# Expert gate and up weights loaded in 4 KB rows, tokens gathered from a plainly ordered copy, pick counts kept in PSUM, and the first refill of the weight ring split into four

## The reference, cut to what matters

```python
def ec_moe(x, w_router, w_gate, w_up, w_down):       # once per depth, DEPTH = 2
    cap = CAPACITY_FACTOR * N // N_EXPERTS            # 2 * 256 // 16 = 32
    aff = jax.nn.softmax(jnp.einsum('bnd,de->bne', x, w_router).astype(jnp.float32), axis=-1)
    gates, idx = lax.top_k(jnp.swapaxes(aff, 1, 2), cap)
    xin = x[bidx, idx]                                # 32 tokens for each of 16 experts
    h = jax.nn.silu(jnp.einsum('becd,edf->becf', xin, w_gate)) * jnp.einsum('becd,edf->becf', xin, w_up)
    out = jnp.einsum('becf,efd->becd', h, w_down) * gates[..., None].astype(x.dtype)
    return jnp.zeros_like(x).at[bidx, idx].add(out.astype(x.dtype))
```

## Time and profile before

| | |
|---|---|
| median of 3 runs | 1518.0 us (1516.62 to 1518.1) |
| the profiled execution | 1516.21 us, of which the profile's span is 1514.4 us |
| PE busy | 1277.8 us (84%) |
| PE weight load busy | 759.9 us (50%) |
| DVE, ACT, POOL busy | 515.0, 235.6 and 325.2 us |
| DMA | 498.93 MB in 88544 packets, mean 329 GB/s |
| chain that ended last | PE 48%, DMA 39%, DVE 3% |

### The profile page before, as it was taken

How to read it: one execution, slowest core, us unless ns; L and a number is a source line. 1 busy time by engine, 2 the same in 40 slices (tenths; PEclk the granted TensorE clock), 3 DMA queues, 4 the chain that set the end, 5 groups by cost and what they waited for, 6 DMA issues and landing times.

```text
span 1514.4 us, 21701 instructions
## 1 busy us (share of the span) xinstructions
PE 1277.8 (84%) x9352; PEld 759.9 (50%) x9352; DVE 515.0 (34%) x982; ACT 235.6 (16%) x490; POOL 325.2 (21%) x278
## 2 busy tenths in 40 slices
PE   8999987668667668999998667777668999999998
PEld 7555534224224234865644224324324975899943
DVE  2686111001001006676311000000002555489894
ACT  2132100001000001351300000000000144212120
POOL 2635000000000004684300000000000654375700
PEclk9999999889889889999999888879989999999999
DMA  9938899999999999845799999999999973835100
GB/s 340 385 111 353 345 427 427 427 428 426 427 428 428 426 426 370 332 167 195 270 427 426 427 428 428 427 426 427 427 427 407 344 235 112 269 121 190 62 0 28
DMA packets 88544, 498.93 MB, mean 329 GB/s; under 512 B 8677, under 2 KB 31649, under 8 KB 64129
## 3 DMA queue, kind: packets, MB, share of 16 engines
q1 hardware_dynamic: 85728, 490.23, 79.8%
q0 software_dynamic: 2720, 7.32, 1.5%
HBM read 496.45 MB, written 1.07 MB: 329 GB/s over the span
## 4 chain that ended last, share of the span: by engine, by line
PE 48%; DMA 39%; DVE 3%; another core or an unknown queue 2%; issue 1%; ACT 0%; SPq 0%; DVEq 0%
DMA weight_ring<-in_moe_w_down 19%; PE bank L950 13%; DMA weight_ring<-in_moe_w_up 10%; PE bank L953 8%; DMA weight_ring<-in_moe_w_gate 6%; PE bank L1252 6%; PE bank L1449 4%; PE bank L1304 3%; DMA phase_room<-in_moe_w_gate 3%; PE bank L1227 3%; PE bank L1319 3%; PE bank L912 2%; PE bank L1418 1%; PE bank L1175 1%
## 5 line engine op out<-in xcount | busy, mean ns | idle before, releaser
L1252 PE MATMUL bank<-weight_ring,x_tok 128*32 128x256 f32 x3328 | 225.7, 422 | 99.8 <-DMA weight_ring<-in_moe_w_up 74.6
L1252 PEld LDWEIGHTS bank<-weight_ring,x_tok 128*32 128x32 f32 x3328 | 109.6, 119 | 212.5 <-issue 84.2
L743 POOL TENSOR_TENSOR weight_ring<-weight_ring 128x512 f32<-128x512 f32 x120 | 163.2, 1390 | 182.0 <-PE bank L950 73.2
L1304 PE MATMUL bank<-weight_ring,xT 128*32 128x512 f32 x864 | 135.4, 757 | 75.6 <-DMA weight_ring<-in_moe_w_down 67.0
L732 POOL TENSOR_TENSOR weight_ring<-weight_ring 128x512 f32<-128x512 f32 x60 | 80.4, 1370 | 451.5 <-DMA weight_ring<-in_w_qkv 438.0
L2312 DVE TENSOR_TENSOR xT<-xT,bank 128x256 f32<-128x256 f32 x32 | 13.5, 421 | 437.4 <-PE bank L1252 437.4
L1319 PE MATMUL bank<-x_tok,xT 128*128 128x512 f32 x256 | 122.8, 623 | 0.0
L2319 DVE COPY x_tok<-bank 128x512 f32<-128x512 f32 x32 | 22.1, 691 | 245.0 <-PE bank L1304 245.0
L1304 PEld LDWEIGHTS bank<-weight_ring,xT 128*32 128x32 f32 x864 | 27.1, 123 | 155.4 <-DMA weight_ring<-in_moe_w_down 76.1
L773 POOL DMA_DIRECT2D phase_room<-in_gla_w_in x1 | 1.0, 953 | 429.4 <-PE bank L1304 429.4
L1319 PEld LDWEIGHTS bank<-x_tok,xT 128*128 128x128 f32 x256 | 48.2, 199 | 84.0 <-issue 84.0
(11 more groups left out here) (319 smaller groups left out, 1619.9 us busy)
## 6 DMA issues: line engine op xcount, KB each, us to landing
weight_ring<-in_moe_w_gate SPq DMA_DIRECT2D x52, 2048.0 KB, 48.4
weight_ring<-in_moe_w_up SPq DMA_DIRECT2D x52, 2048.0 KB, 49.7
weight_ring<-in_moe_w_down SPq DMA_DIRECT2D x52, 2048.0 KB, 48.9
phase_room<-in_moe_w_gate SPq DMA_DIRECT2D x12, 2048.0 KB, 47.0
phase_room<-in_moe_w_up SPq DMA_DIRECT2D x12, 2048.0 KB, 50.3
weight_ring<-in_w_up SPq DMA_DIRECT2D x22, 1024.0 KB, 10.0
phase_room<-in_moe_w_down SPq DMA_DIRECT2D x8, 2048.0 KB, 50.4
weight_ring<-in_gla_w_in SPq DMA_DIRECT2D x6, 2048.0 KB, 23.3
```

Of the source, the lines that this page charges most:

```text
L743: nc.gpsimd.tensor_tensor(b, a, b, ALU.subtract).then_inc(weights_summed[x], 1)
L1252: last = mm(bank[q * CAP:(q + 1) * CAP, 0:S], xinT[:, 4 * r + k, j * CAP:(j + 1) * CAP], w[k][:, q * S:(q + 1) * S], start=(r == 0 and k = ...
L1304: last = mm(PS[i][k * CAP:(k + 1) * CAP, :], hidT[:, 4 * r + k, :], w[k][:, i * 512:(i + 1) * 512], start=(r == 0), stop=(r == 1), skip_gr ...
```

## The change

It has one part for the loads, and four that follow from it or stand at the start of each depth of experts.

1. **Layout.** Partition p of a gate or up tile holds rows k x 128 + p of its half. A load is four pieces of 4 KB for each partition; down stays at 16 KB. `x_hat` becomes a view with contiguous chunks, and the norm's gain and bias columns come from a block that is already in SBUF (four small DVE copies early in the program), so four tiny GpSimd loads go.
2. **Pick counts.** DVE's running sum and mask work on PSUM, with a column of ones that TensorE writes by one extra multiplication.
3. **Filler.** `keep_busy` goes from 19 to 21.
4. **Residual.** ACT scales the second 128 tokens after it has taken its first two chunks of the gather, not before.
5. **First refill.** The tile with index 12 is loaded in four parts of 512 KB, each issued when TensorE has used the row that it replaces.

```diff
+T_REFILL = [TILE_BEFORE.index(base) for base in T_MOE]
...
-    x_hat = acc_t[:, :].rearrange("p (t n k) -> p t k n", t=TT, k=KC)
+    x_hat = acc_t[:, :].rearrange("p (t k n) -> p t k n", t=TT, k=KC)
...
     def arrived(pe, n):
-        pe.wait_ge(landed[SLOT_OF[n]], landings(n))
+        if n in T_REFILL:
+            pe.wait_ge(refilled, 64 * (T_REFILL.index(n) + 1))
+        else:
+            pe.wait_ge(landed[SLOT_OF[n]], landings(n))
...
+        def load_by_rows(n, src):
+
+            layer = T_MOE.index(TILE_BEFORE[n])
+            for k in range(4):
+                if k < 3:
+                    sp.wait_ge(row_used, 3 * layer + k + 1)
+                else:
+                    free(n)
+                sp.dma_start(slot(n)[:, k * D:(k + 1) * D], src[:, k]).then_inc(refilled, 16)
+            sp.sem_inc(landed[SLOT_OF[n]], 16)
...
-            ws = [t[w][layer].rearrange("e (p r k) n -> e r p (k n)", p=P, k=4)
-                  for w in ("moe_w_gate", "moe_w_up", "moe_w_down")]
+            ws = [t[w][layer].rearrange("e (r k p) n -> e r p k n", p=P, k=4) for w in ("moe_w_gate", "moe_w_up")]
+            ws.append(t["moe_w_down"][layer].rearrange("e (p r k) n -> e r p (k n)", p=P, k=4))
...
+                elif n in T_REFILL:
+                    load_by_rows(n, src)
                 elif i < E * TPE - 1:
-                    load(n, src)
+                    load(n, src, slot(n).rearrange("p (k n) -> p k n", k=4) if c < 4 else None)
...
-            for cols, of in ((gain_cols, g), (bias_cols, b)):
-                pool.dma_start(cols, of.rearrange("(p k) -> p k", k=KC)).then_inc(rows_landed, 16)
...
-                last = turn(PS[2][0:E, tt * P:(tt + 1) * P], aff[:, tt, :], ident)
-            last.then_inc(affT_done, 1)
-            keep_busy(19, PS[3], right=consts[:, 0:P])
+                turn(PS[2][0:E, tt * P:(tt + 1) * P], aff[:, tt, :], ident)
+            mm(PS[2][0:E, S:S + 1], ident[0:E, 0:E], ones[0:E, 0:1], start=True, stop=True).then_inc(affT_done, 1)
+            keep_busy(21, PS[3], right=consts[:, 0:P])
...
+                        if e == 0 and c == 0 and r == 0 and k < 3:
+                            last.then_inc(row_used, 1)
...
+            for layer in range(DEPTH):
+                v.tensor_copy(gain_of[layer], norm_cols[:, layer, 0])
+                last = v.tensor_copy(bias_of[layer], norm_cols[:, layer, 1])
...
-            link(v.tensor_tensor_scan(pick, ones[0:E, 0:1].to_broadcast([E, S]), work, 0.0, ALU.mult, ALU.add))
-            v.scalar_tensor_tensor(pick, work, 0.0, pick, ALU.is_lt, ALU.mult).then_inc(slots_ready, 1)
+            count = PS[2][0:E, 0:S]
+            link(v.tensor_tensor_scan(count, PS[2][0:E, S:S + 1].to_broadcast([E, S]), work, 0.0, ALU.mult, ALU.add))
+            v.scalar_tensor_tensor(pick, work, 0.0, count, ALU.is_lt, ALU.mult).then_inc(slots_ready, 1)
```

More of the change, by code:

```diff
@@ L249, in build_in @@
     shift = small[:, 144:146]
-    gain_cols, bias_cols = small[:, 228:236], small[:, 236:244]
+    gain_of, bias_of = (small[:, 228:236], small[:, 88:96]), (small[:, 236:244], small[:, 146:154])
     norm_blocks = room[0:24, 1056:1056 + P]
@@ L398, in build_in @@
     router_landed = sem("router_landed")
+    row_used, refilled = sem("row_used"), sem("refilled")
     router_steps, weighted_done = sem("router_steps"), sem("weighted_done")
@@ L745, in moe_small @@
         def moe_small(layer):
-            pool.wait_ge(rows_landed, 64 * (layer + 1))
+            pool.wait_ge(rows_landed, 32 * (layer + 1))
             for tt in range(TT):
@@ L1657, in moe, with residual @@
         def moe(layer, use):
-            for tt in range(TT):
+            def residual(tt):
                 act.wait_ge(row_scaled, 2 * (TT * layer + tt + 1))
@@ L1662, in moe @@
                 last.then_inc(alpha_x, 1)
+            residual(0)
             base, n0, m0 = T_MOE[layer], E * layer, NG * layer
-            act.wait_ge(rows_landed, 64 * (layer + 1))
+            act.wait_ge(router_steps, 2)
+            gain_cols, bias_cols = gain_of[layer], bias_of[layer]
             act.wait_ge(alpha_x, TT * layer + 1)
@@ L1675, in moe @@
                         last.then_inc(xin_act, 1)
+                        if e == 0 and half == 0:
+                            residual(1)
                 act.wait_ge(tile_used, base + TPE * e + 2)
@@ L1860, in layer_apply @@
                 if use % 2 == 0:
-                    dve.wait_ge(rows_landed, 64 * (use // 2 + 1))
+                    dve.wait_ge(rows_landed, 32 * (use // 2 + 1))
                 else:
@@ L2253, in rms @@
             if tt == 0:
-                dve.wait_ge(*((rows_written, sum(ROUNDS)), (rows_landed, 64 * 2 + 16), (gain_landed, 48))[u])
+                dve.wait_ge(*((rows_written, sum(ROUNDS)), (rows_landed, 32 * 2 + 16), (gain_landed, 48))[u])
             v.scalar_tensor_tensor(acc[:, tt], x_tok[:, tt], inv_spread[:, n:n + 1], gain,
@@ L2288, in moe @@
             base, n0, m0 = T_MOE[layer], E * layer, NG * layer
-            dve.wait_ge(rows_landed, 64 * (layer + 1))
+            dve.wait_ge(router_steps, 2)
+            gain_cols, bias_cols = gain_of[layer], bias_of[layer]
             dve.wait_ge(alpha_x, TT * layer + 1)
```

## The result

The changed kernel takes 1538.99 us (median of 4 runs, 1536.87 to 1539.48) against 1517.31 us (1515.83 to 1518.1) for the kernel before: a ratio of 1.0142, 95% interval 1.0128 to 1.0156. That is 21.7 us slower, where +7.8 was forecast; the direction was right, and the time lies above the range of 1517 to 1534 us. The profiled execution took 1539.07 us with a span of 1537.3, against a span of 1514.4 before.

The account below looks back on a forecast made before the run. The prediction took the experts' load stream, from tile 1's release on, as the bound: +18.4 us for 4 KB pieces and -10.6 for earlier release make +7.8, 1526 us on the median of 1518.0, range 1517 to 1534 us.

Parts of the forecast that it names:

- What bounds the kernel: Both depths' experts: the load stream counts from tile 1's release, then 414 us to the last landing, 4.99 us a tile.
- The cost: 4 KB pieces: Gate and up loads behind the stream's start: 413 GB/s, +0.167 us for each of 110 tiles, +18.4 us.
- Rival A: Expert loads: a deep queue hides the packets' overhead, only the gain is left, 1507.4 us; chance 0.14.
- Rival C: Gather: not faster, since something other than the step makes it slow; 1536 us; chance 0.05.
- Rival D: Gate and up loads: the new pieces run like 2 KB pieces, +56 us, 1563 us; chance 0.03.
- The gain: Contiguous gather and start of each depth: tile 1 free 6.05 and 4.54 us earlier, -10.6 us together.
- the forecast -0.78: Gather's start: running sum -0.91 and extra multiplication +0.13 at the first depth; only +0.13 at the second.
- The fifth edit is worth 1.3 us a depth: First refill by rows: starts 1.35 us earlier, so does not hold back the stream; 1.3 us a depth, within the 10.6.
- rival B: Gather: contiguous instructions run at half clock, 1.6 us a depth lost, 1529 us; chance 0.18.
- The filler: Router's stretch: two more products lie under DVE's pick rounds, at nothing; 0.45 us a depth if they stuck out.
- Edits at nothing: ACT's residual, filler, four DVE copies (under 1.5 us if uncovered) and dropped GpSimd loads, all put at nothing.
- The running sum: DVE before the gather: 0.68 us at both depths with one SBUF operand only, -0.91 at the first depth.

Follow-up runs that it names:

- experiments 3, 5 and 6: Changed kernel with gate and up loaded in 16, 8 and 2 KB pieces respectively, features paired wrongly: 1513.5, 1523.1 and 1570.5 us.
- pieces_16k: Changed kernel with gate and up loaded in 16 KB pieces again, features paired wrongly: 1513.5 us, ratio 0.9967.
- edits_2_to_5: Kernel before with all of the change but its layout part: 1516.76 us, ratio 0.9992.
- experiments 8 and 11: The changed kernel and the kernel of experiment 10, each with its first refill as one whole load: 1540.57 and 1512.48 us.
- gather_alone: Kernel before with contiguous x_hat in the old feature order, written permuted by ScalarE and read permuted by GpSimd; 16 KB pieces: 1516.29 us, ratio 0.9993.
- layout_only: Kernel before with the layout part of the change alone: 1540.29 us, ratio 1.0151.
- permuted_short_filler: Kernel of experiment 10 with less filler, one product for three and 14 for 21: 1509.85 us, ratio 0.9949.
- experiment 4: Changed kernel with the four gain and bias copies made by ScalarE from PSUM instead of VectorE from SBUF: 1534.31 us, ratio 1.0112.
- experiment 12: The same run as permuted_short_filler: kernel of experiment 10 with less filler in the router's stretch, 1509.85 us, ratio 0.9949.
- experiment 10: Changed kernel but with 16 KB pieces, x_hat written permuted by ScalarE and gain columns loaded by GpSimd, no VectorE copies: 1513.26 us, ratio 0.9964.

## Why the prediction was right and wrong

**What bounds the kernel: right.** The difference lies in the release of tile 1 and in the stream behind it; the rest behind the last landing is 348.8 or 348.9 us before and after the change.

**"The cost: 4 KB pieces": the mechanism right, the size too small, and this is the step that failed by most.** It is 5.1 of the 15.1 us that the forecast lacks. Alone it would have left the time at 1526 + 5.1 = 1531 us, inside the range; it took the terms below that stood at nothing, 7.6 us together, to carry it out. The forecast had 0.167 us a tile from a window of 6 us at 413 GB/s. A short window is good to about a percent: the same loads show 415 GB/s from 1396 to 1402 us and 408 from 1395 to 1401. A percent of 427 is a quarter of the whole effect, 18 GB/s from 427 to 409. The steady windows give 0.214, x 110 = 23.5 us; the medians 25.5, with what the clock did in them; the gaps, 427.9 us (mean of eight, 4 KB) against 415.5 (mean of ten with an early release, 16 KB), give 24.9. The Trainium skill's 408.7 GB/s (DMA: Bandwidth & Descriptors, section iDMA fabric, under iDMA vs SDMA), by which the term was estimated at 24 us, agrees: 2.097 MB / (4.911 + 0.214) is 409 GB/s. The prediction could also have had it from its own rows: 387 GB/s at 2 KB is 0.51 us for 56 more pieces an engine, and 24/56 of that is 0.22.

**Rival A, packets cost nothing: excluded** by experiments 3, 5 and 6. The Trainium skill's rule that spoke for it (DMA: Bandwidth & Descriptors, Specifications: line rate from 512 B up) does not hold in this stream: tiles in 4 KB pieces run 4% slower (409 GB/s) and those in 8 KB pieces 1.4%. **Rival C is excluded** too: the 16 gather instructions take 2.05 us. **Rival D**, 4 KB pieces as dear as 2 KB ones, is excluded by the windows at 415; experiment 6 has the 2 KB pieces themselves, 1570.5 us where 1563 was given.

**"The gain": the release as worked out, but two things left out.** The gather's quarters 2 and 3, timeline of the changed kernel:

```profile
157.66 2.05 PE L1243 MATMUL bank<-phase_room,acc 128*128 128x128 f32 x16
```

It is 2.05 for 1.79, and tile 1 is free at g + 8.04 for 7.49, the same at both depths. So 0.5 us a depth of the forecast gain is missing, 1.1 in all. It does not show in the changed kernel's total, by luck: its first mixer happened to run 1.1 us ahead of that of the kernel before already at the products at 48.93 us (50.03 before). In pieces_16k, where the clock was high at both depths, tile 1's refill comes 3.28 and 4.79 us earlier than before, 8.1 in all; with the copies' price, some 10 of the forecast 10.6. That is near, but luck helped here too. From the second logits to the gather its first depth takes 9.98 us for 10.76, the forecast -0.78; its second 9.97 for 10.91, where +0.13 was forecast, since there the kernel before ran at the low clock. Those 0.9 us are not the change's. What the forecast left out:

- *The stream's start.* It took for granted that a microsecond of earlier release is one of earlier landing once the refill goes by rows. In the five kernels with 16 KB pieces and an early release the gap grew from 414 to 415.5 on average, with rows or whole: 1.5 us a depth, 3 us in all. The single values scatter as much: 413.8 to 416.3 among these ten, and edits_2_to_5, with its late release, has 416.0 and 413.9. "The fifth edit is worth 1.3 us a depth" is wrong: experiments 8 and 11 show no worth. Why the rows don't help is not shown; while they alone run in pieces_16k, before tile 1's refill is issued, the queue moves 248 to 287 GB/s at a share of 0.80 to 0.84, so small loads seem to be slow ones.
- *The clock, in another place than rival B's.* Rival B looked for half clock in the gather, where it came in gather_alone's second depth (3.78 us). In the changed kernel's first depth it fell earlier. Windows (PEclk third from the end), then TensorE's timeline:

```profile
144.00:150.00 6.00, 6.00 (x29) 4.82 (x29) 3.44 (x14) 2.53 (x5) 4.08 (x2) 0.60 0.84 352
```

```profile
140.97 2.75 PE L1209 MATMUL bank<-router,xT 128*128 128x16 f32 x16 [0.25 <-ACT xT L1650]
143.56 2.91 PE L873 MATMUL bank<-consts 128*128 128x256 f32 x6
...
146.96 5.80 PE L873 MATMUL bank<-consts 128*128 128x128 f32 x42
152.69 0.29 PE L1231 MATMUL bank<-consts,phase_room 16*128 16x16 f32 x2
153.56 0.71 PE L1243 MATMUL bank<-phase_room,acc 128*128 128x128 f32 x4 [0.58 <-DVE phase_room L2305]
```

  and the same stretch in pieces_16k at a granted clock of 1.00:

```profile
142.24 1.96 PE L1209 MATMUL bank<-router,xT 128*128 128x16 f32 x16 [0.25 <-ACT xT L1650]
144.05 1.54 PE L873 MATMUL bank<-consts 128*128 128x256 f32 x6
...
146.21 4.96 PE L873 MATMUL bank<-consts 128*128 128x128 f32 x42
151.36 0.29 PE L1231 MATMUL bank<-consts,phase_room 16*128 16x16 f32 x2 [0.19 <-DVE phase_room L2300]
152.22 1.94 PE L1243 MATMUL bank<-phase_room,acc 128*128 128x128 f32 x15 [0.58 <-DVE phase_room L2305]
```

From the second logits to the gather are 12.59 us at the low clock and 9.98 at the high one: 2.6 us. Of these 0.8 are the logits' own (2.75 us for 1.96). The filler, put at nothing, is most of the rest: at the low clock it ends after what it was to cover (VectorE has the picks ready at 151.64 + 0.41 = 152.05 us, and TensorE comes for them at 152.69). Only the lower of its two places is longer by the change: layout_only, with 38 instructions for 42 and the clock as low, has 11.91 us, 0.68 less. In the kernel before, the first depth's dip came after the gather's start, where it hardly shows. At the second depth both kernels lose some there, and the stretch is equal (10.96 and 10.91). What moves the dip is open: in the profiles of ten of the twelve experiments it lies before the gather at one depth or at both, in gather_alone in the gather, in pieces_16k nowhere near. One thing does sort the first depth: there it lies before the gather in all six profiles with pieces under 16 KB, the changed kernel's among them, and in two of the eight with 16 KB pieces (edits_2_to_5 and permuted_short_filler). With one profile of each kernel that is a hint that the pieces have a part in it, and not more.

**"Edits at nothing": the copies were not.** They were bounded at 4 x 0.37 = 1.5 us, from an operation that reads PSUM, and cover was assumed. They took 1.23, 0.16, 1.23 and 0.16, 2.78 us together, TensorE waited 1.76, and the stretch of the first mixer around them grew by 1.9 (experiment 4). From the x24 products to the second logits of that depth are 92.0 us in place of 90.0, the 2.0 of the sum below. ACT's residual and GpSimd's dropped loads were rightly nothing. The running sum took 0.69 us, where 0.68 was forecast.

The sum, on the profiled executions: +7.8 forecast, +5.1 for the steady price of pieces, +3.0 for the stream's start, +2.0 for the copies, +2.6 for the clock make 20.5; measured 22.9. The remaining 2.4 lie in the gaps: 428.5 on average, where these terms give 414.05 + 1.5 + 55 x 0.214 = 427.3. The gaps of the kernels with 4 KB pieces differ among each other by 3.1 us (426.3 to 429.4), and I leave that open.

## What to carry to other kernels

Where the end of a kernel hangs on a saturated load stream, price a change of layout by its count of contiguous pieces, and take the price from two piece sizes or a long window: a short window's percent of error times a hundred tiles was larger than any other single term here. If the engines want another order of the data, let a compute engine write it so and leave the pieces long, but then follow what else that engine's new pace delays: the faster gather was worth nothing by itself, and something (0.9964) in the kernel where the operation that a late GpSimd row held up had an operand in PSUM. That kernel had three more edits, so which of them brought the gain is argued from the timelines and not shown by a run. And filler that keeps TensorE busy can itself be on the path at the low clock: with less of it experiment 12 was the fastest, though not clear of experiment 10.

## What the runs showed of the hardware

- A piece more costs a DMA engine 8.7 to 9.2 ns in a full stream, by the steady windows, at 8, 4 and 2 KB alike (427, 423, 415 and 399 GB/s in the mix with one third of the tiles at 16 KB). How deep the queue is, six loads or ten, changes nothing (ratio 0.9989, 427 GB/s).
- With 512 pieces to a 2 MB load SP is held at its issues with about five loads outstanding (landings 24 to 29 us behind the issue in place of 47 to 50); with 256 pieces the landings are 34 to 38 us behind, with 1024 pieces 19 to 25.
- A 128 x 8 copy from SBUF to SBUF on VectorE took 1.23 us twice and 0.16 us twice, in turn, while GpSimd worked all along (54.40 to 62.6 us). A 16 x 256 operation with SBUF operands alone took 2.38 us in place of 0.41 under a GpSimd row; with one operand in PSUM it took 0.41 under the same row.
- ScalarE's centring of 128 x 1024 values takes 2.23 us permuted and 1.23 plain; GpSimd's row operation 2.87 for 2.35.
